# Third stage of a two-layer transformer kernel: its projections and its last product on f32r split halves

## The reference

```python
def odd_mixer(x, ...):
    q_c, k_c, v_c, q_d, k_d, v_d, r_d, g_d = jnp.split(x @ w_in, ODD_SPLITS, axis=-1)
    # differential attention, 4 heads, two softmaxes each
    s = where(dist >= 0, q_c @ k_c.T * dh ** -0.5 + bias, -inf)
    p = softmax(s)
    o_c = rms_norm((p[:, 0] - lam * p[:, 1]) @ v_c, diff_norm_w) * (1.0 - lam_init)
    # gated linear attention (GLA), 4 heads, decay per column of q and k
    log_a = log_sigmoid(g_d @ gla_w_gate + gla_b_gate) / 16
    o_d = rms_norm(gla_chunked(q_d * 64 ** -0.5, k_d, v_d, log_a), gla_norm_w) * silu(r_d)
    return jnp.concatenate([o_c, o_d], -1) @ w_out
```

## Time and profile before

| | |
|---|---|
| three runs | 1815.8, 1819.53, 1820.54 us, median 1819.53 |
| the profiled execution | 1823.2 us, its span 1821.5 us |
| TensorE, weight loads | busy 1736.7 us (95%), 1280.2 us (70%) |
| VectorE, ScalarE, GpSimd | busy 976.5 (54%), 641.2 (35%), 230.2 us (13%) |
| mean granted clock of TensorE | 0.98 |

### The profile page before, as it was taken

One profiled execution on the slowest core, in us unless ns is written; L12 is line 12 of the kernel. 1 busy time (PEld: TensorE's weight loads), 2 busy tenths in 40 slices (PEclk: granted clock), 3 DMA queues, 4 the chain that ended last, 5 costly groups with the idle time before them and its releaser, 6 DMA issues. The chain is left out here.

```text
span 1821.5 us, 25863 instructions
## 1 busy us (share of the span) xinstructions
PE 1736.7 (95%) x10464; PEld 1280.2 (70%) x10464; DVE 976.5 (54%) x1806; ACT 641.2 (35%) x1078; POOL 230.2 (13%) x217
## 2 busy tenths in 40 slices
PE   9999999999999989999999989999899999899987
PEld 8788875799886544999888764434489898544434
DVE  1176664688541575787456663233267867533223
ACT  1025322467430224666446431111144455311111
POOL 0000000163110130353002302000000200010000
PEclk9899999999999889999999999999999999999999
DMA  8422186445434595455344659999934555799995
GB/s 306 149 94 93 60 339 249 185 181 213 162 139 162 185 362 232 161 213 187 139 144 177 247 202 420 420 420 420 371 121 160 185 208 208 308 419 420 420 420 230
DMA packets 51853, 443.05 MB, mean 243 GB/s; under 512 B 5900, under 2 KB 6160, under 8 KB 9104
## 3 DMA queue, kind: packets, MB, share of 16 engines
q1 hardware_dynamic: 47664, 426.79, 60.1%
q0 software_dynamic: 2480, 8.92, 1.3%
q10 hardware_dynamic: 1584, 5.61, 0.8%
HBM read 440.25 MB, written 1.05 MB: 242 GB/s over the span
## 5 line engine op out<-in xcount | busy, mean ns | idle before, releaser
L88 ACT ACTIVATE arena<-ps 128x384 f32<-128x384 f32 (+5 forms) x233 | 101.6, 436 | 546.3 <-PE ps L82 344.1
L82 PE MATMUL ps<-ringx,arena 128*64 128x512 f32 x1056 | 276.2, 594 | 7.9 <-DMA ringx<-in_mg 3.5
L82 PE MATMUL ps<-xsplit_f,wsplit_f 128*128 128x256 f32 x2112 | 257.1, 284 | 3.5 <-ACT xsplit_f L88 2.7
L82 PEld LDWEIGHTS ps<-xsplit_f,wsplit_f 128*128 128x128 f32 x2112 | 255.5, 193 | 5.5 <-ACT xsplit_f L88 4.2
L82 PE MATMUL ps<-ring,arena 128*64 128x512 f32 (+1 forms) x704 | 228.8, 598 | 9.5 <-DMA ring<-in_mu 6.0
L91 DVE TENSOR_TENSOR wsplit_f<-ring,wsplit_f 128x1024 fp32r<-128x1024 f32 x132 | 180.6, 1372 | 70.4 <-ACT wsplit_f L88 70.4
L82 PEld LDWEIGHTS ps<-ringx,arena 128*64 128x64 f32 x1056 | 89.6, 137 | 170.3 <-issue 156.3
L82 PE MATMUL ps<-xTs,ring 128*128 128x256 f32 (+1 forms) x960 | 188.3, 356 | 2.3 <-ACT xTs L88 1.8
L82 PEld LDWEIGHTS ps<-xTs,ring 128*128 128x128 f32 x960 | 163.0, 193 | 24.5 <-issue 6.6
L88 ACT ACTIVATE wsplit_f<-ring 128x1024 fp32r<-128x1024 f32 x132 | 138.2, 1051 | 57.5 <-PE ps L82 56.5
L82 PEld LDWEIGHTS ps<-ring,arena 128*64 128x64 f32 (+1 forms) x704 | 78.6, 148 | 104.8 <-issue 89.2
(11 more groups left out here) (197 smaller groups left out, 2425.0 us busy)
## 6 DMA issues: line engine op xcount, KB each, us to landing
ring<-in_ada SPq DMA_DIRECT2D x24, 2048.0 KB, 8.0
ring<-in_wu SPq DMA_DIRECT2D x22, 2048.0 KB, 8.1
ringx<-in_mg SPq DMA_DIRECT2D x44, 1024.0 KB, 20.8
ringx<-in_mu SPq DMA_DIRECT2D x44, 1024.0 KB, 23.8
ringx<-in_md SPq DMA_DIRECT2D x44, 1024.0 KB, 26.1
ring<-in_md SPq DMA_DIRECT2D x24, 1024.0 KB, 25.5
ring<-in_mg SPq DMA_DIRECT2D x24, 1024.0 KB, 20.7
ring<-in_mu SPq DMA_DIRECT2D x24, 1024.0 KB, 23.9
```

The lines of the kernel that those rows point to most:

```text
L82: return self.e.matmul(o, l, r, start=start, stop=stop, skip_group_check=True)
L88: return self.e.activation(o, i, f, **k)
```

## The change

Of the third stage, tiles 4 to 15, `vc`, `vd` and the last product go to f32r on split halves; tiles 0 to 3 and the gate stay float32.

- Chunks: `ODD_CH` has 28 of 1024 columns: 0 to 3 `wo` 1, 4 to 7 `wo` 2, 8 to 11 `wov` 0, 12 to 15 `wo` 3, 16 to 19 `wov` 1, 20 to 27 `woo`. `low_half` writes in place, over the weight in its slot; the high halves have four buffers of their own. `wo` is laid out tile by tile in HBM.
- Order: three `ada` pieces go ahead of `DIFF`; `AMONG` has 18 entries, two of them empty; `SPLIT_AT` says at which filler which chunk is split. Low halves 20 to 27 are GpSimd's, 20 to 23 behind GLA levels 5 and 6, ahead of the next memset.
- Transfers: `woo` 0 goes ahead of the last five `ada`; every transfer's slot is named in `BESIDE`, as the slot of a transfer before it.
- The input of the last product is split too, by pairs of row blocks (`high_out` on ScalarE, `low_out` on VectorE).
- `ffn_first` waits for GpSimd's last low half.
- The causal mask is added to the table `TP` at the end of stage one and no longer in this stage, and x of this stage is transposed into the place of the output, `O.xT`.

```diff
-AMONG = [("po", 12), ("ada", 0), ("po", 13), ("ada", 1), ("po", 14), ("po", 15), ("vd", 0), ("ada", 2), ("vd", 1)] \
-    + [("ada", k) for k in range(3, ADA)]
+AMONG = [("po", 12), ("po", 13), ("ada", 3), ("po", 14), ("po", 15), ("ada", 4), ("vd", 0), ("vd", 1)] \
+    + [("ada", k) for k in range(5, ADA)] + [None, None]
+
+SPLIT_AT = {0: (15,), 3: (16, 17), 4: (18,), 5: (19,), 10: (20, 21), 11: (22,), 12: (23,)}
...
+ODD_CH = chunks("T", ("wo", 1), ("wo", 2)) + chunks("R", ("wov", 0)) + chunks("T", ("wo", 3)) + chunks("R", ("wov", 1)) \
+    + chunks("D", ("woo", 0), ("woo", 1))
...
-    out += [("wo", 0), ("wo", 1), ("wo", 2), ("wov", 0), ("wo", 3)] + ada[:3] + [("wov", 1)] + ada[3:]
-    out += [("woo", 0), ("woo", 1)] + ffn(1)
+    out += [("wo", 0), ("wo", 1), ("wo", 2), ada[0], ("wov", 0), ada[1], ada[2], ("wo", 3), ("wov", 1)] + ada[3:7]
+    out += [("woo", 0)] + ada[7:] + [("woo", 1)] + ffn(1)
...
-ELSEWHERE = {("ada", 2, 2): 2, ("wov", 1): 0}
+BESIDE = {("ada", 2, 0): ("wo", 0), ("wov", 0): ("wo", 1), ("ada", 2, 1): ("ada", 2, 0), ("ada", 2, 2): ("ada", 2, 1),
+          ("wo", 3): ("wo", 2), ("wov", 1): ("wov", 0), ("ada", 2, 3): ("ada", 2, 2), ("ada", 2, 4): ("ada", 2, 3),
+          ("ada", 2, 5): ("wo", 3), ("ada", 3, 0): ("ada", 2, 4), ("woo", 0): ("wov", 1), ("ada", 3, 1): ("ada", 2, 5),
...
# on TensorE
-            for n in range(9, 12):
-                proj_T(("wo", 2), "po", n, n % 4, 3)
-            proj_rows(("wov", 0), "vc", 512)
+            tile_split(2, 5, "po", 9)
+            ada_piece(1, 1)
+            for n in (10, 11):
+                tile_split(2, n - 4, "po", n)
+            rows_split(2, 8, "vc")
+            ada_piece(1, 2)
...
+            down_split(2, ("dn", 2), 20, lambda f: O.ohi[:, f, :], lambda f: O.olo[:, f, :], lambda f: v("osplit", f // 2),
+                       {2: gla_sums})
...
# VectorE
+            for i in range(3):
+                low_half(2, i)
+            for n in range(4):
+                q_tile(n)
+            for i in range(3, 7):
+                low_half(2, i)
+            gate_inputs()
...
+                for i in SPLIT_AT.get(k, ()):
+                    if i < 20:
+                        low_half(2, i)
...
# ScalarE
+            for n in range(2):
+                a.wait_ge(*v("gl_out", n))
+                high_out(2 + n)
+            for i in range(25, 28):
+                high_half(2, i)
...
# GpSimd
+                if i in (5, 6):
+                    for c in range(2):
+                        low_half(2, 10 + 2 * i + c)
+            for i in range(24, 28):
+                low_half(2, i)
+            g.note("early", 2)
             norm(2)
```

More of the change, by code:

```diff
@@ L276, in all_slots @@
         else:
-            if name in ELSEWHERE:
-                i = ELSEWHERE[name]
-            else:
-                i = turn % SLOTS
-                turn += 1
+            if name in BESIDE:
+                i = out[BESIDE[name]][0]
+            else:
+                i = min(range(SLOTS), key=lambda k: (LOADS.index(last[k]) if k in last else -1, k))
+            turn = i + 1
         used[i] = used.get(i, 0) + 1
@@ L482, in chunk, with halves @@
         lo = PLACE[src][0] * 4096 + 1024 * c
-        parts = ring[:, lo:lo + 1024], ringhi[:, i % 4, :], ringlo[:, lo:lo + 1024]
+        if n == 2:
+            parts = ring[:, lo:lo + 1024], O.rhi[:, i % 4, :], ringall[:, lo:lo + 1024]
+        else:
+            parts = ring[:, lo:lo + 1024], ringhi[:, i % 4, :], ringlo[:, lo:lo + 1024]
         return [ap.rearrange("p (k n) -> p k n", k={"T": 8, "R": 2, "D": 1}[kind]) for ap in parts]
+    def halves(n, i):
+        return (g if n == 2 and i >= 20 else v)("split", n, i)
     def half_arrived(name, h):
+        if name[0] not in NARROW:
+            return arrived(name)
         n, count, _ = PLACE[name]
@@ L575, in emit @@
         O.qd, O.kdT, O.kdt, O.Sg = (rows(m.take(256), 2, 128) for _ in range(4))
+        low_part = m.top
+        m.take(2048)
+        O.rhi = fr(st, "odd_high", 4, 1024)
+    with ExitStack() as st:
+        st.enter_context(nc.sbuf_tensor("below_odd_x", [128, low_part], F32))
+        O.xtl = fr(st, "odd_xlow", 8, 256)
+    with ExitStack() as st:
+        O.ohi, O.olo = (fr(st, f"odd_out{i}", 8, 256) for i in range(2))
     with ExitStack() as st:
@@ L782, in down_part, with x_low, rows_half @@
                 t.note("used", src)
+        def x_low(n):
+            return O.xtl if n == 2 else xtl
+        def rows_half(n, i, tag, h):
+            b, tk = bank(tag, h), slice(h * 128, h * 128 + 128)
+            for c in range(4):
+                _, hi, lo = chunk(n, i + c)
+                t.wait_ge(*halves(n, i + c))
+                for k in range(2):
+                    for q, (w, xx) in enumerate(((hi, xth), (lo, xth), (hi, x_low(n)))):
+                        r = mm(b, xx[:, 2 * c + k, tk], w[:, k, :], c + k + q == 0, (c, k, q) == (3, 1, 2))
+                if h and c < 3:
+                    r.then_inc(s_pe, t.did())
+                    t.note("part", n, i + c)
+            r.then_inc(s_pe, t.did(tag, h))
+            if h:
+                t.note("part", n, i + 3)
+                t.note("used", CHUNKS[n][i][0])
         def tile_split(n, i, tag, j, ring=R8):
@@ L805, in rows_split @@
                 _, hi, lo = chunk(n, i + c)
-                t.wait_ge(*v("split", n, i + c))
+                t.wait_ge(*halves(n, i + c))
                 for h in range(2):
@@ L827, in down_split @@
                 _, hi, lo = chunk(n, i0 + f)
-                t.wait_ge(*v("split", n, i0 + f))
+                t.wait_ge(*halves(n, i0 + f))
                 t.wait_ge(*ready(f))
@@ L2776, in odd @@
             a.note("lam")
-            for n in (10, 11):
-                tile(n)
+            high_half(2, 9)
+            tile(10)
+            high_half(2, 10)
+            tile(11)
+            for i in range(11, 15):
+                high_half(2, i)
             Bq = O.Bc.rearrange("p (n t m) -> p n t m", n=2, t=2)
@@ L3102, in row_applied, with low_half @@
                 g.tensor_tensor(x[:, h, :], x[:, h, :], lnp[:, 1024:2048], ALU.add).then_inc(s_pool, g.did("gx", n))
+        def low_half(n, i):
+            part, hi, lo = chunk(n, i)
+            g.wait_ge(*a("hi", n, i))
+            g.tensor_tensor(lo, part, hi.bitcast(F32), ALU.subtract).then_inc(s_pool, g.did("split", n, i))
         def norm(n):
```

116 lines of the change are left out of this document (74 added, 42 removed).

## The result

The changed kernel takes 1843.8 us (median of four runs, 1839.5 to 1846.5), the kernel before, run beside it, 1817.9. The ratio is 1.0132, 95% interval 1.0113 to 1.0152: slower by 24 us by the ratio (the two medians lie 25.9 apart), where 18 were forecast. The profiled execution has a span of 1841.3 us against 1821.5.

A forecast was written before the change was run, and what follows sets the result against it. TensorE is 95% busy, but the stage's middle was taken as bound by a VectorE, ScalarE, GpSimd chain. Steps reach +17.8 us: 1823.2 + 18 = 1841, less 3.7 for the runs' median, 1837.5 us; 8-in-10 range 1819 to 1854.

The forecast's parts named there:

- TensorE: what goes: TensorE time saved by split halves: tiles 7.4 us, two row products 5.8, last product 5.7; 19 us in all.
- Rival 1: TensorE stays the bound, waits in `DIFF` stay at 14.4 us and all 19 us count: 1801 us, chance 0.13.
- Step A: Stage start up to `DIFF`: three pieces added, a wait for piece 1 and slowed first halves outweigh savings, +2.7 us.
- Step B: First two pairs: low halves 15 and 18 delay VectorE's normalising; +8.8 us, third pair 11.5 us later.
- Step C: Last two pairs: GpSimd's low halves delay the last memset, +4.8 us, and fourth pair's normalising, +1.5; last products +17.8.
- The term of the ports: VectorE's normalising of the fourth pair slowed beside GpSimd's low halves: +1.5 us, bounds 0 and 4.
- Step D: From last level's products to the last product: new high part 0.6 us, low part 0.7; start +15.2 us.
- rival 3: Shared ports: GpSimd halves at 3.1 us or more, start stall at upper bound, clock 0.9; 1846 us, chance 0.20.
- Step E: Last product: TensorE waits for GpSimd's halves 25 to 27, the 5.7 us saved is waited away; end +14.9 us.
- Step F: Norm: `ffn_first` waits for GpSimd's last half; second transpose at 743.7 us instead of 725.86, +17.8.
- Rival 2: GpSimd's halves are hidden, VectorE being late anyway or a half costing nearer 1.2 us: 1826 us, chance 0.17.

The follow-up runs named there:

- e1: Changed kernel with GpSimd's low halves 20 to 23 moved behind its last level sum; 1833.7 us, ratio 1.0073.
- e2: Changed kernel with low halves 24 to 27 written by VectorE instead of GpSimd; 1838.9 us, ratio 1.0102.
- e3: Changed kernel with low halves 15 and 18 one entry later and 16 one earlier, away from the normalisations; 1832.7 us, ratio 1.0073.
- e8: Changed kernel with everything back in float32, keeping only the new order of transfers, slots and pieces and the mask's new place; 1825.1 us, ratio 1.0032.
- e7: Changed kernel with the last product back in float32, tiles and row products still on split halves; 1826.2 us, ratio 1.0034.
- e9: e8 with `woo` 0 loaded behind all pieces and the slot of `wov` 1 given to piece 7; 1824.6 us, ratio 1.0030.
- e12: e7 with low halves away from the normalisations, GpSimd's scaling of x behind low half 6, and `woo` 0 behind all pieces; 1815.6 us, ratio 0.9974.
- e11: Changed kernel with useless TensorE products before the last level, before the last product and in its three waits; 1843.9 us, ratio 1.0130.

## Why the prediction was right, and where it was too small

The direction, the chain and the places of the waits were right; the sum was 6 us short. By the steps, in the profiled execution and from the stage's first transpose:

- **TensorE: what goes.** Forecast 19 us. The page shows 14.6 us less busy, which holds products that the low clock stretched. The terms were right where the clock was full: the 48 products of the row product `vc` took 11.1 us (580.53 to 591.62), forecast 11.02. Rival 1 (all 19 count) is refuted by the wait of the first pair, 4.3 us where it needed under 2.
- **Step A**, forecast +2.7, measured +4.6 (67.7 to 72.3). The stall at the start was smaller (1.86 + 0.17 us of waiting, forecast 3.4). The wait for the transfer of piece 1 was larger: 2.33 us in place of 0.9, and the piece behind it took 3.38 us instead of 1.92 at the low clock. The same code in e1, e2 and e3 came out at +1.9, +2.1 and +1.4, with a wait of 0.77 to 1.55 us for piece 1 and 1.92 for the piece, so the forecast lies within what single traces show.
- **Step B**, forecast +8.8, measured +8.4, and 13.9 us of waiting forecast in two pairs; the six waits there are 4.32, 1.03, 2.36, 4.82, 0.89 and 0.30, 13.7 in all. VectorE's third pair starts 13.0 us late by the common clock, forecast 11.5; the difference is step A's. e3 shows that these waits are the halves' places. In the forecast halves (3.4 + 9.4 = 12.8 us) stood against 11.9 of TensorE time saved, and the moved pieces and `vd` came on top (6.3 + 0.9 + 5.5 - 2.1 = 10.6). e8 has neither halves nor savings, and its third turn is late by 8.3 us: these last terms were about right, and the order had to be named as a cause of its own, which no rival does.
- **Step C**, forecast +6.3, measured +8.0 (VectorE's last products at +21.0). The memset cost 4.96, forecast 4.8. The term of the ports was mis-sized: 1.5 forecast, and the two operations took 2.46 + 2.34 - 0.29 - 0.35 = 4.2 us more. GpSimd's half itself is 2.33 us, forecast 2.4.
- **Step D**, forecast -2.6, measured -0.7: the four sums took 3.78 us instead of 1.88, at a granted clock of 0.50 (699.5 to 703.6). The forecast had put the low clock in rival 3 alone. It belongs in the sum wherever a wait of several us is forecast.
- **Step E**, forecast -0.3, measured +2.7. The last product lasted 32.0 us, forecast 28.9, through 4.2 us of waits and two stretches of low clock.
- **Step F**, forecast +2.9, measured +2.3.

Steps C to F add up to 6.3 us in the forecast and to 12.3 in the traces; A and B to 11.5 and 13.0. So the terms that failed in size are E with D (4.9 us short together): the last product, forecast as a gain of 5.7 us waited away, is the dearest part. By the differences of runs the change with it costs 17.8 us more than e7 without it (24.0 - 6.2), against those 6.3. The difference was hidden in part by luck: the forecast carries the +11.5 of the third pair to the stage's end, where e7, without the last product, has only +8.4 left. Why it falls is not shown; fewer pieces in the last pairs would do it. Rival 2 (GpSimd's halves hidden) is refuted by e1 and e2. The measured 1843.8 us lies 0.8 above the forecast's own bracket (1829 to 1843) and inside rival 3's (1842 to 1856), but not for rival 3's reasons: GpSimd's halves took 2.33 us and not 3.1 or more, and the stall at the start cost 2.0 us and not 7. Of its three terms only the low clock came, and to it the two slowed VectorE operations of step C.

The Trainium skill (SBUF — State Buffer, "SBUF: two separate sides") says that of two operations that both want the shared port pair of VectorE and GpSimd, the one that starts first keeps it for the whole instruction. This case's traces agree in their ends: VectorE's TENSOR_SCALAR of 677.67 ends at 680.13 and GpSimd's first half at 680.02, the next operation at 682.50 and the second half at 682.35. The second VectorE operation starts 0.14 us behind its GpSimd half; the first starts 0.02 us ahead of its own and is held up all the same, and spans on GpSimd are too rough to say which was first. Here the price was 2.2 and 2.0 us, nearly a whole GpSimd instruction (2.33) for each of the two; at the stage's start it was less, 8.3 us for five operations.

What stays open: e9 is 3.4 us over before in its stage (201.8 against 198.4). TensorE's waits in it are 4.7 us longer in all: two for VectorE's share of the pieces (`tmpn`) take 4.3 us against 1.1, and one of 1.60 for GpSimd's last level sum is new. Why they come is not shown; the places of the pieces are the explanation left, and putting pieces 0 to 2 back was not tried. Nor was the last product tried on split halves with its halves on VectorE and a float32 first part. And the sizes of the steps A to F rest on one trace of each kernel.

## What to carry to other kernels

Where an engine writes its work in order, ask of each inserted operation what it waits for and who is behind it: two low halves, each one entry later, were worth 10 us, more than the 7.4 that the split of all tiles was to save. A cause of loss tested in a badly placed version says little of the well placed one: the first half gained nothing in e7 and 10 us in e12 against e9. TensorE time is only worth saving where TensorE sets the end; in a stage whose tail is a chain, the halves of the last product come on that chain. Judge a change of several parts part by part: here the last product made 13.5 to 17.8 of the 24 us (7.4 with all halves well placed) and the new order 5.8. The first half, rightly placed, is the only part that pays, and with the new order it leaves 0.3% (e12, interval 0.07 to 0.45%).

## What the runs showed of the hardware

- A VectorE operation of 128x128 that needs 0.29 us took 2.46 and one of 0.35 took 2.34 beside GpSimd's 128x1024 subtractions. Copies out of PSUM beside such subtractions kept their 0.42 (e1, four in 2.00 from 700.46), and reciprocals beside GpSimd's level sums their 0.17. Five low parts and halves took 13.3 us beside GpSimd's scaling and 5.0 without.
- GpSimd subtracts 128x1024 float32 in 2.33 us, VectorE in 1.23.
- TensorE's granted clock fell from 1.00 to 0.50 around waits of very different length, and four sums that take 1.88 us at the full clock took 3.78 behind a wait of 5.9 us, 3.03 behind one of 6.9 (e2) and 3.14 behind one of 1.9 (e1). Six idle products that ran ahead of a remaining wait of 3.0 us did not keep the clock up for the sums behind it (0.50); three ahead of the last product and two in each of its three waits did (0.50 to 1.00 from 711 to 714 and from 731.7 to 734).
- TensorE at a full clock in the last product (e11) gave 1.4 us in the trace and nothing that the median of four runs can show: executions differ by more.
